# Fifteen of the token mix's sixteen gate groups placed beside the grouped heads' attention, with norms applied in three instructions a row

## The reference, cut to what matters

```python
def rms_norm(x):
    return xf * lax.rsqrt(jnp.mean(xf * xf, -1, keepdims=True) + NORM_EPS)
def modulate(x, shift, scale):
    return rms_norm(x) * (1 + scale) + shift
for l in range(2):
    x = x + 0.5 * g1 * swiglu(modulate(x, sh1, sc1), ...)
    x = x + g2 * token_mix(modulate(x, sh2, sc2), ...)
    x = x + 0.5 * g3 * swiglu(modulate(x, sh3, sc3), ...)
# token_mix(u): two attentions read u, then a gated merge
    o_a = nsa_attention(...)     # 8 grouped heads, two softmax branches + a compressed one
    o_b = mla_attention(...)     # 8 latent heads, one causal softmax
    g_a, g_b = jnp.split(u @ w_in[:, 1976:], 2, axis=-1)
    y = sigmoid(g_a) * (o_a @ w_branch_a) + sigmoid(g_b) * (o_b @ w_branch_b)
    return y @ w_out
```

## Time and profile before

| | |
|---|---|
| median of three executions | 3555.81 us |
| the profiled execution | 3571.1 us |
| its span, first to last instruction | 3569.3 us |
| its mean granted TensorE clock | 0.975 |
| attentions of m0 | about 548 to 672 us of the span |
| gated merge of m0 up to the output projection | 672 to 804 us |

### The profile page before, as it was taken

How to read it: one execution, slowest core, us unless ns; L and a number is a source line. 1 busy time by engine, 2 the same in 40 slices (tenths; PEclk the granted TensorE clock), 3 DMA queues, 4 the chain that set the end, 5 groups by cost and what they waited for, 6 DMA issues and landing times.

```text
span 3569.3 us, 40894 instructions
## 1 busy us (share of the span) xinstructions
PE 3455.7 (97%) x16646; PEld 2777.9 (78%) x16646; DVE 1800.9 (50%) x3132; ACT 1237.3 (35%) x2064; POOL 286.5 (8%) x238
## 2 busy tenths in 40 slices
PE   8999999999999999999899999999999999999999
PEld 6888776787888788877667878887778777878887
DVE  7666457645566733334674443334453665354433
ACT  4222337523222322223573232224322444124322
POOL 0000121002000200021200100012011000020000
PEclk9999999999999999999899999999999999899999
DMA  6565221133565533232102322322221223132332
GB/s 235 207 210 185 99 79 37 40 106 101 190 219 195 175 97 102 92 101 92 59 1 83 103 83 85 111 81 93 66 77 61 76 68 117 31 100 81 98 106 77
DMA packets 120217, 376.36 MB, mean 105 GB/s; under 512 B 13280, under 2 KB 28000, under 8 KB 120032
## 3 DMA queue, kind: packets, MB, share of 16 engines
q1 hardware_dynamic: 120032, 373.76, 32.2%
HBM read 371.61 MB, written 2.10 MB: 105 GB/s over the span
## 4 chain that ended last, share of the span: by engine, by line
PE 89%; DVE 6%; ACT 3%; issue 1%; POOL 1%; DMA 0%; SPq 0%; POOLq 0%; ACTq 0%; DVEq 0%
PE ps L435 25%; PE ps L436 25%; PE ps L437 25%; PE ps L638 2%; PE ps L544 2%; PE ps L657 1%; PE ps L478 1%; PE ps L485 1%; PE ps L469 1%; PE ps L471 1%; PE ps L470 1%; DVE s_wl L1393 1%; ACT s_wh L917 0%; ACT s_tmp L951 0%; POOL s_small L2061 0%
## 5 line engine op out<-in xcount | busy, mean ns | idle before, releaser
L1393 DVE TENSOR_TENSOR s_wl<-s_raw,s_wh 128x1024 fp32r<-128x1024 f32 (+3 forms) x645 | 708.3, 1100 | 867.3 <-ACT s_wh L917 865.2
L435 PE MATMUL ps<-s_uh,s_wh 128*128 128x512 f32 x2696 | 1075.1, 399 | 36.9 <-DVE s_ul L1427 23.9
L436 PE MATMUL ps<-s_uh,s_wl 128*128 128x512 f32 x2696 | 1060.0, 393 | 0.0
L437 PE MATMUL ps<-s_ul,s_wh 128*128 128x512 f32 x2696 | 1059.6, 393 | 0.0
L917 ACT ACTIVATE s_wh<-s_raw 128x1024 fp32r<-128x1024 f32 (+3 forms) x645 | 588.2, 913 | 742.1 <-PE ps L437 555.3
L435 PEld LDWEIGHTS ps<-s_uh,s_wh 128*128 128x128 f32 x2696 | 513.2, 190 | 155.5 <-issue 31.8
L436 PEld LDWEIGHTS ps<-s_uh,s_wl 128*128 128x128 f32 x2696 | 513.4, 190 | 107.9 <-issue 2.7
L437 PEld LDWEIGHTS ps<-s_ul,s_wh 128*128 128x128 f32 x2696 | 512.0, 190 | 108.7
L437 PE MATMUL ps<-s_fl,s_wh 128*128 128x512 f32 x960 | 378.2, 394 | 0.0
L435 PE MATMUL ps<-s_fh,s_wh 128*128 128x512 f32 x960 | 378.2, 394 | 0.0
L436 PE MATMUL ps<-s_fh,s_wl 128*128 128x512 f32 x960 | 378.2, 394 | 0.0
(11 more groups left out here) (405 smaller groups left out, 3673.4 us busy)
## 6 DMA issues: line engine op xcount, KB each, us to landing
s_raw<-w SPq DMA_DIRECT2D x616, 512.0 KB, 3.6
s_raw<-w SPq DMA_DIRECT2D x96, 192.0 KB, 2.4
s_raw<-w SPq DMA_DIRECT2D x64, 256.0 KB, 2.6
s_raw<-w SPq DMA_DIRECT2D x19, 128.0 KB, 2.1
s_x<-x SPq DMA_DIRECT2D x4, 512.0 KB, 6.2
out<-s_x SPq DMA_DIRECT2D x8, 256.0 KB, 2.2
s_raw<-w SPq DMA_DIRECT2D x4, 420.0 KB, 4.0
s_crow<-crow SPq DMA_DIRECT2D x2, 512.0 KB, 3.4
```

Of the source, the lines that this page charges most:

```text
L435: TE.matmul(o, w_hi(i, k), h, start=first, stop=False)
L436: TE.matmul(o, w_lo(i, k), h, start=False, stop=False)
L437: return TE.matmul(o, w_hi(i, k), l, start=False, stop=last)
L1393: V.tensor_tensor(wl[w][:, 0:n], raw[t % NRAW][:, 0:n], wh[w][:, 0:n].bitcast(F32), SUB).then_inc(*s_lo.up(("lo", t)))
```

## The change

- **Order.** `attention_pairs()` lists the 16 latent steps first, the 32 grouped ones after.
- **Gates beside attention.** The first 15 gate groups are cut into quarters of two rows k (6 matmuls each). In each of the grouped steps t = 16 to 45, TensorE issues one quarter after the scores and one after the transposes: 60 quarters. The 16th group (B, m = 7) is issued whole after the attentions. Gate groups use PSUM banks 2 and 3, so grouped scores use only banks 0 and 1.
- **Places.** ScalarE writes the tanh of the gates to the tiles `s_mq` and `s_mk` (free after the latent heads, now called sA and sB); the merged y goes to `s_uh`, `s_ul`. VectorE's merge takes four instructions a row m instead of six: (tanh + 1) times the branch in one, the factor 0.5 later.
- **Norms.** A row takes three instructions: VectorE multiplies x, scale and factor; ScalarE adds the shift and writes fp32r; VectorE adds the shift and subtracts.
- **GpSimd's clears** wait for the last row of the mix's norm.
- **Tables.** The mask is loaded early, `s_dist` after the latent projections.

```diff
@@ def attention_pairs():
-    u = [("nsa", hh, i, br) for hh in range(4) for i in range(4) for br in range(2)]
-    return u + [("mla", j, i, 0) for j in range(4) for i in range(4)]
+    u = [("mla", j, i, 0) for j in range(4) for i in range(4)]
+    return u + [("nsa", hh, i, br) for hh in range(4) for i in range(4) for br in range(2)]
+FIRST_NSA = 16
+FILLED = 15
+def gate_pieces(t):
+    return [(n // 4, n % 4) for n in (2 * (t - FIRST_NSA), 2 * (t - FIRST_NSA) + 1) if 0 <= n < 4 * FILLED]
@@ TensorE, def mix(l):
+            def piece(n, quarter):
+                m, x_ = n // 2, "AB"[n % 2]
+                g = ("g" + x_, st, m)
+                if quarter == 0:
+                    gate_now["mix"] = get(f"g{x_}{l}", 0, 128 * m), take(g, 2 + n % 2)
+                i, o = gate_now["mix"]
+                for k in (2 * quarter, 2 * quarter + 1):
+                    ins = three(o[:, :], i, k, uh[:, k, :], ul[:, k, :], k == 0, k == 7)
+                if quarter == 3:
+                    ins.then_inc(*s_pe.up(("w", i), ("ps", g)))
...
-                    o = [take(("S", (st, 2 * t + g)), 2 * (t % 2) + g) for g in range(2)]
+                    o = [take(("S", (st, 2 * t + g)), 2 * (t % 2 if kind == "mla" else 0) + g) for g in range(2)]
...
+                for n in gate_pieces(t)[0:1]:
+                    piece(*n)
                 if 0 <= t - 2 < len(pairs):
                     for n in (2 * t - 4, 2 * t - 3):
                         turn((st, n), 4 + n % 2, mP[n % 6], 128 * pairs[t - 2][2] + 128)
+                for n in gate_pieces(t)[1:2]:
+                    piece(*n)
...
-            ring[1] = 0
+            for quarter in range(4):
+                piece(15, quarter)
+            ring[1] = 4
             for m in range(8):
                 for x_, h_, l_ in (("A", oAh, oAl), ("B", oBh, oBl)):
-                    fm(("g" + x_, st, m), f"g{x_}{l}", 8, m, uh, ul, ("u", st))
                     fm(("w" + x_, st, m), f"w{x_.lower()}{l}", 4, m, h_, l_, ("o" + x_, st))
@@ ScalarE, def apply
-                SC.activation(t0[:], t0[:], ACT.Identity, bias=0.0 if shift is None else shift(k), scale=scale(k)).then_inc(*s_act.up(("af", st, k)))
-                act.wait_ge(*s_act.now())
-                SC.activation(dst[:, k, :], t0[:], ACT.Copy).then_inc(*s_act.up(("uh", st, k)))
+                if shift is None:
+                    SC.activation(dst[:, k, :], tmp[k % 4][:], ACT.Copy).then_inc(*s_act.up(("uh", st, k)))
+                else:
+                    SC.activation(dst[:, k, :], tmp[k % 4][:], ACT.Identity, bias=shift(k), scale=1.0).then_inc(*s_act.up(("uh", st, k)))
@@ VectorE, def apply
-                    V.tensor_tensor(tmp[k % 4][:], src[:, k, :], more[:] if after_k and k else bank(g)[:], MUL).then_inc(
+                    V.scalar_tensor_tensor(tmp[k % 4][:], src[:, k, :], scale(k), more[:] if after_k and k else bank(g)[:], MUL, MUL).then_inc(
...
+                    V.scalar_tensor_tensor(dst_l[:, k, :], tmp[k % 4][:], shift(k), dst_h[:, k, :].bitcast(F32), ADD, SUB).then_inc(*s_dve.up((*key, k)))
@@ GpSimd, def mix(l):
+            pool.wait_ge(*s_dve["u", st, 7])
             PO.memset(kc[:], 0.0).then_inc(*s_pool.up(("z1", st)))
@@ SyncE
-            tab(f"dist {st}", dist[:], A["dist"])
+            tab(f"mask {st}", mmask[:], A["mask"])
...
             sp.wait_ge(*s_pe["latent", st])
-            tab(f"mask {st}", mmask[:], A["mask"])
+            tab(f"dist {st}", dist[:], A["dist"])
```

More of the change, by code:

```diff
@@ L82, in plan @@
             fm(f"gA{l}", 8, m)
+            fm(f"gB{l}", 8, m)
+        for m in range(8):
             fm(f"wa{l}", 4, m)
-            fm(f"gB{l}", 8, m)
             fm(f"wb{l}", 4, m)
@@ L345, in col @@
         return cst[:, a + i:a + i + n]
+    sA, sB, yh, yl = mq, mk, uh, ul
     ident, ones = col("ident", 0, 128), col("ones", 0, 128)
@@ L1066, in mix @@
                 if h == 4:
-                    apply(("ckv", st), 2, ch, lambda k: col(f"kvn{l}", k))
+                    apply(("ckv", st), 2, ch)
                 for h2 in {5: (1, 2), 6: (3, 4), 7: (5, 6, 7)}.get(h, ()):
@@ L1077, in mix, with gate @@
             act.wait_ge(*s_pe["latent", st])
+            def gate(n):
+                m, x_ = n // 2, "AB"[n % 2]
+                act.wait_ge(*s_pe["ps", ("g" + x_, st, m)])
+                SC.activation((sA if n % 2 == 0 else sB)[:, m, :], bank(("g" + x_, st, m))[:], ACT.Tanh, scale=0.5).then_inc(
+                    *s_act.up(("g" + x_, st, m), frees=("g" + x_, st, m)))
             for t in range(len(pairs) + 3):
@@ L1085, in mix @@
                         SC.activation(p[:, 0:L], p[:, 0:L], ACT.Exp, bias=two(n, 0), scale=-1.0, accum_out=two(n, 1)).then_inc(*s_act.up(("e", (st, n))))
+                for n, quarter in gate_pieces(t):
+                    if quarter == 0:
+                        get(f"g{'AB'[n % 2]}{l}", 0, 128 * (n // 2))
                 if 0 <= t - 2 < len(pairs):
@@ L1092, in mix @@
                         SC.activation(mT[n % 4][:, 0:L], bank(("T", (st, n)))[:, 0:L], ACT.Copy).then_inc(*s_act.up(("pt", (st, n)), frees=("T", (st, n))))
+                for n, quarter in gate_pieces(t - 1):
+                    if quarter == 3:
+                        gate(n)
                 if 0 <= t - 3 < len(pairs):
@@ L1640, in mix @@
             dve.wait_ge(*s_pe["latent", st])
-            dve.wait_ge(*table(f"dist {st}"))
             for t in range(len(pairs) + 1):
+                for n, quarter in gate_pieces(t):
+                    if quarter == 0:
+                        get(f"g{'AB'[n % 2]}{l}", 0, 128 * (n // 2))
                 if t < len(pairs):
```

97 lines of the change are left out of this document (50 added, 47 removed).

## The result

The changed kernel takes 3533.32 us, the median of four executions (3531.60 to 3534.23). The kernel before took 3559.74 us, the median of four executions, the three above and one more. The ratio on record is 0.9919, with a 95% interval from 0.9907 to 0.9932: 0.8% faster. (The two medians alone give 0.9926, inside that interval.) The forecast was 3538 us, 0.5% faster, from 3525 to 3553. The profiled execution took 3532.56 us, its span 3530.8.

The account below looks back on a forecast made before the run. TensorE, busy 97% of the span, was taken as the bound, so only its idle, low-clock or wasteful time could win. Terms 0 + 6.8 + 3.2 + 1.4 + 4.3 + 2 = 17.7 us took 3555.8 to 3538 us, range 3525 to 3553.

Parts of the forecast that it names:

- the likeliest case: Whole kernel: 3538 us, between 3531 and 3545; chance 0.39.
- Gates beside the grouped heads: Grouped steps: idle time won, 2.7 us a mix, equals 60 entries into full-height matmuls, 2.7 us; net 0, -4.6 to +1.5.
- Cover: Attentions and merge: two score banks, the 16th gate group and the merge cause TensorE no wait; cost 0.
- Start of the attentions: First attention steps: waits for slopes and half clock go; gain 3.4 us a mix, 6.8 in all, from 1.3 to 5.
- the six-to-four saving: Merge: VectorE's four instructions a row instead of six win nothing, since TensorE stays the bound.
- Norm rows: Path to TensorE's first row: 0.5 us for each of six modulated norms, 0.65 for s and up; 3.2 us taken.
- Clears: Mix norm's diagonals: without GpSimd's clears beside them, 0.7 us a mix, 1.4 for two.
- Latent projections: cq and ckv rows end earlier, 2.15 us a mix, 4.3 in all; clock staying up adds 2.
- Smaller gain: Rival: entries at 0.11 us and the clock falling at the start leave a 5 us gain, 3551 us; chance 0.15.
- Slow by two banks: Rival: TensorE waits for score banks in all 60 filled steps; at 1 us a step 3598 us; chance 0.04.
- More hidden idle in the grouped steps: Rival: gates fill gaps between small matmuls that records understate, 12 us more, 3526 us; chance 0.25.
- The third block's half clock: Rival: the third block falls to half clock in timed runs too, 13.7 us lost, 3552 us; chance 0.17.

Follow-up runs that it names:

- experiment 2: Changed kernel with all 16 gate groups whole behind the attentions and grouped scores in four banks instead of two; 3541.86 us, ratio 0.9937.
- experiment 5: Kernel before with only the order changed: latent heads first, mask loaded early; 3558.22 us, ratio 0.9988.
- experiment 6: Kernel before with only the norms changed to three instructions a row, small norms too; 3553.30 us, ratio 0.9968.
- experiment 10: Changed kernel with both gate quarters of a step after the transposes, none after the scores; 3532.06 us, ratio 0.9913.
- experiment 4: Changed kernel with the 60 gate quarters spread over all attention steps, one ahead of the first scores, latent scores over three banks; 3529.82 us, ratio 0.9899.
- experiment 9: Changed kernel with both gate quarters of a step after the scores, none after the transposes; 3541.90 us, ratio 0.9940.
- experiment 8: Changed kernel with 1248 unused bytes after the constants and 64 ahead of the later tiles, so large tiles start at multiples of 1024 bytes; 3520.59 us, ratio 0.9882.
- experiment 7: Changed kernel with 64 unused bytes per partition ahead of the feed-forward, mix and third-block tiles; 3513.66 us, ratio 0.9861.
- experiment 11: Changed kernel with 64 unused bytes after the constants, moving all tiles behind them together; 3542.78 us, ratio 0.9940.

## Why the prediction was right, and where it was off

**The total.** 3533.3 us lies in the range and within the likeliest case's own bounds, 3531 to 3545. The gain was larger than forecast: the sum was 17.7 us, the stretches of the first two layers and the norms gained 27.6 us, the medians 26.4. That the time came so near is in part luck: the forecast started from the median of three executions, 3555.8 us, and from 3559.7 us the same sum would have said 3542. Of the 9.9 us above the sum, 3.0 lie in the norms, 0.9 between first rows and first scores, and 6.0 from the first scores on.

**Gates beside the grouped heads: right in the net, by a balance.** Net 0 was forecast, 0.6 and 0.9 us a mix were measured (experiment 2). The size of an entry was taken well after transposes (0.03) and too low after scores (0.06 against 0.11), and the slower pace inside a quarter was not in it. My estimate from these rows is 30 x 0.11 + 60 x 4 x 0.005 = 4.5 us paid a mix instead of 2.7, so 5.1 to 5.4 us won instead of 2.7: both sides were too small.

**Cover: right.** Two score banks cost 0.02 us a step without the gates' cover; the 16th group covers a wait of 2.16 us; the merge has no wait of TensorE.

**Start of the attentions: right, a little low.** 3.4 us a mix forecast, 4.0 us by the order alone. The clock stays up in the changed kernel; in the one of experiment 5 it fell in one of two mixes, as in 4 others of the kernels with this order, which was the lower end of my range.

**A term that was mis-sized** is the merge, which I had at nothing ("the six-to-four saving is worth nothing"). That sentence holds for VectorE. But the merged y moved from tiles of its own into `s_uh` and `s_ul`, and with it the output projection's 192 matmuls from 0.2333 to 0.2267 us. Windows of TensorE from its first to the next norm's sums, before and after:

```profile
804.34:849.13 44.79, 44.79 (x193) 1.00 0.32 102
```

```profile
795.04:838.58 43.54, 43.54 (x194) 1.00 0.35 114
```

(The counts take in a neighbour or two of the 192.) That is 1.25 us a mix, 2.5 in all. In m0 the 6.8 us of the stretch are 4.0 of order, 1.25 of this, 0.6 of the gates' place, and 1.0 that stays open: 0.7 of it stands in the attention part between experiments 5 and 2. In the former GpSimd's slopes run beside VectorE's first scalings (0.73 us instead of 0.48), and TensorE's idle time in the first 10 us adds up to 1.8 us instead of 1.2. I did not test that apart.

**Norm rows: right in kind, low in size.** 0.63 us for a modulated norm instead of 0.5, 0.7 for s, and 1.5 for up (0.7 to 1.5 in the traces of the other kernels with this part). The 0.5 took the one ScalarE instruction that is left at 0.81 us, as long as the old one with scale and shift; with the shift alone it takes 0.72 us, the mean of 48. Whether the earlier start is worth half, because the first rows run at 1.2 GHz, the runs can't tell: the 370 us of a feed-forward vary by 1 to 3 us between kernels that don't touch them. **Clears:** 0.7 us a mix forecast, 0.7 (m0) and 1.1 (m1) measured against the kernel before and 1.5 against experiment 6 (m0).

**Latent projections: right, by a balance.** 4.8 us forecast for the stretch, 5.7 measured. The stop of 2.62 us went to 1.31 us as said, the clock's fall of 3.4 us behind it is gone. Two new stops of 1.5 and 1.1 us came (1.32 and 0.90 us idle by the rows), which I had not seen: the chain of VectorE now meets GpSimd's addition the other way round.

**The rivals.** Smaller gain: no. Slow by two banks: no. More hidden idle in the grouped steps, 12 us: 1.5 us net of it came in the changed kernel, and 5.4 us with all quarters after the transposes (experiment 10 against 2), so its mechanism is real, at about half its size and with another placement. (The 10 us more of experiment 4 lie for more than half in the latent steps and ahead of them.) The third block's half clock: the spell of 27.3 us did not come in the changed kernel. The third block took 1125.6 us in the profiled execution before and 1112.2 after, of which the norms are 2.2; the stretch with the spell gained 10.5 us, where I had counted 13.7. It came in experiment 9, with no edit near it, and for 17.1 us in experiments 5 and 8. So a total of this kernel carries 4 to 13 us that no edit of the third block explains; executions of the kernel before alone differ by 13 us. The stretches without it gained 27.6 us, which is why I take the 26.4 us of the medians as the change's own.

## What to carry to other kernels

Ask of each tile that a matmul reads where it starts: in the long runs here input and weights that stood alike within 128 bytes streamed at 0.2267 us, others at 0.2333, and 64 unused bytes were worth 20 us, three quarters of what the whole change gained. Measure it for each tile, since the latent projections went the other way. Work that fills gaps wins where the engine waits, and between small instructions only what its own entries leave: put a piece into each step that waits, behind transposes rather than behind scores. And when a total moves, compare stretches first, since a clock that falls elsewhere can be larger than what you changed.

## What I had not expected of the hardware

- The two paces of the same matmul, 0.2333 and 0.2267 us at 2.4 GHz. They depend on input and weights relative to each other (experiments 7, 8, 11), with remainders of 32, 96 and 0 bytes by 128 tried and none else. They are not the whole rule: `s_qh` and `s_ch` have 0.229 to 0.233 us in every kernel.
- The same 93 matmuls of the third block run in 27.30 us at a granted clock of 0.50 in two kernels, and in others at a higher one:

```profile
3033.66:3050.40 16.74, 16.74 (x93) 13.65 (x93) 1.56 (x3) 3.06 (x5) 3.42 (x4) 0.90 0.02 9
```

This is the changed kernel, at that place. By their order in the program, the same matmuls take 15.1 to 16.7 us from first start to last in ten kernels, 22.2 and 24.0 in experiments 8 and 5, and 27.1 in these two. TensorE was busy throughout in all three rows, and what decides it these runs don't show.
- A gap of 0.09 to 0.10 us, counted as in experiment 10, at a change to or from matmuls of 64 rows or 64 columns, three a step, with or without gates between. The Trainium skill (TensorEngine Tiling, Key Properties) has a change of mode drain TensorE; the three gaps agree, and full-height gates add none. By that rule alone the gates would have been worth 2 us a mix. They were worth 0.6 to 0.9 in the changed kernel, where after scores the first matmul takes 0.11 us more, and 2.7 with all quarters after transposes.
